# Reading the moving tiles of the weight products backwards, and spacing one activation buffer by 32 bytes per tile

## The reference

```python
def conv_glu_ffn(h, w_gate, w_up, conv_w, conv_b, w_down):
    g = h @ w_gate
    ...
    return (jax.nn.silu(gc) * (h @ w_up)) @ w_down

x = x + jnp.concatenate([y_pool, y_mla, y_mem], axis=-1) @ w_o[l]
x = x + conv_glu_ffn(rms_norm(x, g_ffn[l]), w_gate[l], w_up[l], conv_w[l], conv_b[l], w_down[l])
```

## Time and profile before

| what | value |
|---|---|
| median of 3 runs | 1601.56 us (1597.0 to 1602.5) |
| span of the profiled execution, first to last instruction | 1599.0 us |
| the profiled execution's own time around the span | not given; the median of the runs is 2.6 us more than the span |
| TensorE matmul busy | 1573.0 us (98%) |
| VectorE busy | 1154.1 us (72%) |
| ScalarE busy | 862.4 us (54%) |
| moved by DMA | 331 MB, mean 207 GB/s |

### The profile page before, as it was taken

The page is one execution under the profiler, slowest core; times in us unless marked ns, Lnnn a source line. Parts: engine busy times, 40 slices in busy tenths (PEclk is TensorE's granted clock), DMA queues, the critical chain, the costliest instruction groups (busy, mean ns, idle before and its releaser), DMA issues.

```text
span 1599.0 us, 24289 instructions
## 1 busy us (share of the span) xinstructions
PE 1573.0 (98%) x9650; PEld 1400.7 (88%) x9650; DVE 1154.1 (72%) x1696; ACT 862.4 (54%) x1321; POOL 151.6 (9%) x164
## 2 busy tenths in 40 slices
PE   8998999989999999999999999999999999999999
PEld 6787889988999999988799888888888888888887
DVE  6797867877778886759778777777777777455544
ACT  6855546767665555655556454544444444444442
POOL 0000000321221220034213000000000000000000
PEclk9999999999999999999999999999999999999999
DMA  9999975533457774343244545555455454555552
GB/s 373 369 343 349 365 285 209 188 114 121 180 189 267 285 272 179 132 158 132 97 144 178 189 170 199 184 186 210 172 197 191 179 211 175 205 199 185 198 196 105
DMA packets 47825, 331.02 MB, mean 207 GB/s; under 512 B 5281, under 2 KB 6689, under 8 KB 8417
## 3 DMA queue, kind: packets, MB, share of 16 engines
q1 hardware_dynamic: 45184, 312.20, 53.5%
q0 software_dynamic: 2240, 17.04, 2.8%
q10 hardware_dynamic: 290, 0.25, 0.1%
HBM read 327.37 MB, written 2.10 MB: 206 GB/s over the span
## 4 chain that ended last, share of the span: by engine, by line
PE 89%; DVE 5%; DMA 3%; ACT 2%; issue 1%; POOL 0%; SPq 0%; ACTq 0%; DVEq 0%; POOLq 0%
PE ps L1173 20%; PE ps L1174 11%; PE ps L1169 9%; PE ps L1170 8%; PE ps L1171 8%; PE ps L1228 5%; PE ps L1227 5%; PE ps L1226 5%; PE ps L1216 4%; PE ps L1217 3%; PE ps L1218 3%; DVE wl L1916 2%; DMA raw<-in_wts 1%; DMA xs<-in_xN 1%; PE ps L1384 1%; PE ps L1351 1%
## 5 line engine op out<-in xcount | busy, mean ns | idle before, releaser
L1916 DVE TENSOR_TENSOR wl<-raw,wh 128x1024 fp32r<-128x1024 f32 x512 | 626.2, 1236 | 282.4 <-ACT wh L1519 281.9
L1519 ACT ACTIVATE wh<-raw 128x1024 fp32r<-128x1024 f32 x512 | 531.3, 1054 | 377.2 <-PE ps L1228 130.6
L1173 PE MATMUL ps<-hA,wh 128*128 128x512 f32 x1408 | 488.7, 390 | 0.0
L1174 PE MATMUL ps<-hA,wl 128*128 128x256 f32 x1408 | 397.0, 282 | 0.0
L1173 PEld LDWEIGHTS ps<-hA,wh 128*128 128x128 f32 x1408 | 264.2, 188 | 55.3
L1174 PEld LDWEIGHTS ps<-hA,wl 128*128 128x128 f32 x1408 | 266.1, 189 | 0.0
L1169 PE MATMUL ps<-hA,wh 128*128 128x256 f32 x752 | 219.5, 292 | 0.0
L1170 PE MATMUL ps<-hA,wh 128*128 128x256 f32 x752 | 211.7, 282 | 0.0
L1171 PE MATMUL ps<-hA,wl 128*128 128x256 f32 x752 | 211.7, 282 | 0.0
L1169 PE MATMUL ps<-hB,wh 128*128 128x256 f32 x576 | 164.4, 285 | 0.8 <-DVE work L2362 0.4
L1170 PE MATMUL ps<-hB,wh 128*128 128x256 f32 x576 | 161.1, 280 | 0.0
(11 more groups left out here) (303 smaller groups left out, 2077.9 us busy)
## 6 DMA issues: line engine op xcount, KB each, us to landing
raw<-in_wts SPq DMA_DIRECT2D x256, 1024.0 KB, 4.8
raw<-in_ada SPq DMA_DIRECT2D x36, 1024.0 KB, 6.1
side<-in_ada POOLq DMA_DIRECT2D x12, 1024.0 KB, 8.5
work<-in_memN SPq DMA_DIRECT2D x2, 1024.0 KB, 8.9
xs<-in_xN POOLq DMA_DIRECT2D x1, 2048.0 KB, 20.6
xs<-in_xT POOLq DMA_DIRECT2D x2, 1024.0 KB, 7.8
out_rows<-xs SPq DMA_DIRECT2D x8, 256.0 KB, 2.4
wp<-in_dt SPq DMA_DIRECT2D x8, 128.0 KB, 2.7
```

What stands on the lines that cost most here:

```text
L1173: e.matmul(ps[bank][:, :], w1, hl, start=first, stop=False)
L1174: i = e.matmul(ps[bank][:, T:2 * T], w2, hl[:, 0:T], start=False, stop=last)
L1519: e.activation(wh[:, h % WS, :], raw[:, n % RAW, part * HALF:(part + 1) * HALF], ACT.Copy).then_inc(s_hi)
L1916: e.tensor_tensor(wl[:, h % WS, :], src, wh[:, h % WS, :].bitcast(F32), ALU.subtract).then_inc(s_lo)
```

## The change

Every moving tile of the weight products is addressed from its last column with a step of -1. Where the weights are stationary, the output tile in PSUM is addressed backwards too, so each column lands where it did. Where the weights move, the output stays forward, and the host stores each group of 512 weight columns in reverse in HBM instead (`standing` tells which groups). The loads of stationary blocks keep their addresses and their step.

The second edit puts 8 elements (32 bytes) between the K-tiles of `hA` and `hA2` (class `Slots`), so that tile kt begins at 128 + 32 kt or 160 + 32 kt modulo 512; `hB` and `hB2` are not spaced. The 480 bytes for it come out of the mask table, which is stored without its unused halves (576 in place of 1024 bytes per partition), and out of a gap ahead of `hB`, which is aligned to 512 in place of 2048 bytes. Everything behind `hA` moves by 480 or 512 bytes, `work` by 64.

The number and the order of the instructions on all five engines are the same; the one row that differs is the load of the masks.

```diff
+class Slots:
+    def __getitem__(self, at):
+        rows, kt, w = at
+        first = kt * (512 + SHIFT)
+        return self.tensor[rows, first + w.start:first + w.stop]
...
-        hA = sb("hA", [P, KT, 512], F32R)
+        hA = Slots(sb("hA", [P, KT * 512 + SHIFT * (KT - 1)], F32R))
...
-        at[0] += (hA_off - at[0]) % 2048
+        at[0] += (hA_off - at[0]) % 512
...
-        mk = sb("mk", [P, len(LEVELS), P], U8, 1)
+        mk = sb("mk", [P, P + 64 * (len(LEVELS) - 1)], U8, 1)
...
-        hA2 = nc.alloc_sbuf_tensor_at("hA2", [P, KT, 512], F32R, offset=hA_off + 32)
+        hA2 = Slots(nc.alloc_sbuf_tensor_at("hA2", [P, KT * 512 + SHIFT * (KT - 1)], F32R, offset=hA_off + 32))
...
-                hl = moving[buf][:, kt % KT, :]
+                hl = moving[buf][:, kt % KT, 0:512]
...
-                    e.matmul(po, w1, hl[:, 0:T], start=first, stop=False)
-                    e.matmul(po, w1, hl[:, T:2 * T], start=False, stop=False)
-                    i = e.matmul(po, w2, hl[:, 0:T], start=False, stop=last)
+                    po, hi, lo = (x[:, ::-1] for x in (po, hl[:, 0:T], hl[:, T:2 * T]))
+                    e.matmul(po, w1, hi, start=first, stop=False)
+                    e.matmul(po, w1, lo, start=False, stop=False)
+                    i = e.matmul(po, w2, hi, start=False, stop=last)
                 else:
-                    e.matmul(ps[bank][:, :], w1, hl, start=first, stop=False)
-                    i = e.matmul(ps[bank][:, T:2 * T], w2, hl[:, 0:T], start=False, stop=last)
+                    e.matmul(ps[bank][:, ::-1], w1, hl[:, ::-1], start=first, stop=False)
+                    i = e.matmul(ps[bank][:, T:2 * T][:, ::-1], w2, hl[:, 0:T][:, ::-1], start=False, stop=last)
...
-                w1, w2 = (w[:, h % WS, c % 2 * 512:c % 2 * 512 + 512] for w in (wh, wl))
+                w1, w2 = (w[:, h % WS, c % 2 * 512:c % 2 * 512 + 512][:, ::-1] for w in (wh, wl))
...
+            if not standing(kind, wn, cols) and j % 4 == 3:
+                wts[nw, :, (j - 3) * P:(j + 1) * P] = wts[nw, :, (j - 3) * P:(j + 1) * P][:, ::-1].copy()
```

More of the change, by code:

```diff
@@ L27 @@
 LANES = 6
+SHIFT = 8
 SETS = (tuple(c + P * j for c in (6144, 6656, 2048, 2560) for j in range(4)),
@@ L832, in order, with __init__ @@
     return o
+class Slots:
+    def __init__(self, tensor):
+        self.tensor = tensor
+    def __getitem__(self, at):
+        rows, kt, w = at
+        first = kt * (512 + SHIFT)
+        return self.tensor[rows, first + w.start:first + w.stop]
 class Counts:
@@ L1141, in _ @@
                 elif b[0] == "consts":
-                    e.dma_start(mk[:].rearrange("p a b -> p (a b)"), msk).then_inc(s_mask, 16)
+                    e.dma_start(mk[:], msk).then_inc(s_mask, 16)
                     e.dma_start(cs[:, P:], cst[:, P:]).then_inc(s_const, 16)
@@ L1182, in m @@
                 for j, kt in enumerate(kts):
-                    w1, w2 = wh[:, h % WS, j * 512:(j + 1) * 512], wl[:, h % WS, j * 512:(j + 1) * 512]
+                    w1, w2 = (w[:, h % WS, j * 512:(j + 1) * 512][:, ::-1] for w in (wh, wl))
                     if fresh[j]:
@@ L1203, in chunk @@
                     c = 2 * pair + i
-                    w1, w2 = wh[:, h % WS, i * 512:(i + 1) * 512], wl[:, h % WS, i * 512:(i + 1) * 512]
+                    w1, w2 = (w[:, h % WS, i * 512:(i + 1) * 512][:, ::-1] for w in (wh, wl))
                     if kt == kts[0]:
@@ L2042, in pick @@
                         src = bank[:, :].rearrange("p (a w) -> p a w", a=4)
-                        mask = mk[:, 0, :].unsqueeze(1).broadcast_to([P, 4, P])
+                        mask = mk[:, 0:P].unsqueeze(1).broadcast_to([P, 4, P])
                     else:
@@ L2048, in pick @@
                         src = bank[:, 0:T].rearrange("p (a n w) -> p a n w", a=4, w=h)
-                        mask = mk[:, li, 0:64].rearrange("p (n w) -> p n w", w=h).unsqueeze(1).broadcast_to([P, 4, n, h])
+                        mask = mk[:, P + 64 * (li - 1):P + 64 * li].rearrange("p (n w) -> p n w", w=h).unsqueeze(1).broadcast_to([P, 4, n, h])
                     e.copy_predicated(dst, mask, src).then_inc(mark(t, "dve", ("p", li)))
@@ L2561, in constants, with standing @@
             m[:, n, 0:64] = (s // (2 * h) == late // (2 * h)) & (s % (2 * h) < h)
-    return c, m.reshape(P, -1)
+    return c, np.concatenate([m[:, 0]] + [m[:, n, 0:64] for n in range(1, len(LEVELS))], 1)
+def standing(kind, wn, cols):
+    if kind == "m" or wn == "w_down_2":
+        return False
+    return wn != "w_kv_up_2" or cols[0] % 256 == 0
 def kernel(**inputs):
```

## The result

The kernel became slower: 1619.3 us (median of 4 runs, 1616.9 to 1621.9) against 1601.4, a ratio of 1.013 with a 95% interval of 1.011 to 1.014. The forecast was 1547, the range 1518 to 1640 held the time, and the case to which I gave the most chance was wrong in its sign.

A forecast was written before the change was run, and what follows sets the result against it. Behind 200 us the kernel was taken as a TensorE matmul queue, number times spacing. Reading backwards gave -55 us, spacing, output, reversal and masks 0: 1601.6 - 55 = 1547 us, range 1518 to 1640.

The forecast's parts named there:

- the case to which I gave the most chance: Whole kernel: faster by 55 us, to 1547 us within 1535 to 1568; chance 0.43.
- The columns' own 106.7 and 213.3 ns: TensorE matmuls: at the full 2.4 GHz clock, 256 columns take 106.7 ns and 512 take 213.3.
- The excess is the same for 256 and 512 columns, so it belongs to something that happens once per matmul: Matmul spacings: excess about 13.5 ns in both shapes, assigned to loading the next stationary block; 113 us in all.
- Collisions: SBUF: the excess is the load's read colliding with the moving tile's; at most 91 us can go.
- reading backwards: Moving tiles: running the load's way gives a third as many collisions, two thirds of excess above 2.5 ns gone; -55 us.
- The spacing of the K-tiles: `hA` tiles: spacing changes each tile's distance to the weight block, not the number of passings; 0 us, within 5.7 either way.
- The sign that was named for a distance that matters beyond the direction: Timeline after: `hA` tiles whose spacing goes with kt would show that distance matters beyond direction; no size given.
- The output backwards, the reversal, the masks: PSUM output, host's weight reversal and mask load: columns land in their old places, reversal precedes launch; 0 us.
- A: Moving tile held behind the load, in all `hB2` and some `hA` matmuls: +45 us, 1647; chance 0.23.
- B: Excess is the load's own share in any direction; only `hA` products gain, about -6 us, 1596; chance 0.17.
- C: All matmuls: excess falls to the transposes' 2.5 ns because spacing keeps reads apart, -83 us, 1519; chance 0.12.
- D: Backward tiles move at half pace; if only backward-output matmuls do, 876 us more, about 2480; chance 0.05.

The follow-up runs named there:

- mb3_kinds: None of the kernel's work: matmul groups varying type, distance and address against the next loaded block; bf16 512 columns took 215.8 ns, 256 took 109.2.
- mb2_maps: None of the reference's work: the kernel's pair and triple patterns at distances in 16-byte steps, then columns 128 to 512; forward pair 346.7 ns at 32, triple 360.0 at 0.
- mb1_pairs: None of the reference's work: 2472 matmuls in groups of 32 varying direction, distance and block; 512 columns at distance 0 took 226.7 ns forward, 233.3 backward.
- e_back: Against the kernel before: everything read backwards, in the old layout, K-tiles not spaced; 1612.4 us, ratio 1.009 (1.007 to 1.011).
- e_space: Against the kernel before: K-tiles of `hA` spaced, masks as in the changed kernel, all read forwards; 1602.3 us, ratio 1.002 (1.001 to 1.004).
- mb4_starts: None of the kernel's work: 16 triples or pairs follow one matmul of 16 to 512 columns; at distance 192, spacings of 113.3 and 117.8 ns.

## Why the prediction was wrong, point by point

- *What bounds the kernel*: right. The time is the number of matmuls times their spacing; both before and after TensorE is full behind 200 us, and its waits stayed as short (the longest 5.5 us in both).
- *The columns' own 106.7 and 213.3 ns*: right. No row of before shows them; mb3_kinds does (106.6 ns for 256 more bf16 columns), and it shows the 2.5 ns over them too. Plain float32 goes at half that pace in the kernel before: four matmuls of 256 columns in 1.03 us (L1384 at 622.73), (1.03 - 0.38)/3 = 217 ns each, against 109 for the 128 of the transposes, so 0.84 ns a column against 0.42. The load's 107 was my estimate from the transposes; the nearest to it is L101 of mb2_maps, where fp32r matmuls of 128 and of 192 columns, with a block of 128 loaded beside each, both take 112 ns ((2.40 - 0.27)/19 and (2.73 - 0.27)/22).
- *"The excess is the same for 256 and 512 columns, so it belongs to something that happens once per matmul"*: this is the step that failed. mb2_maps shows 12 ns over at 256 columns and 19 at 512 in the same place, mb3_kinds 2.5 ns in bf16 with the same number of columns and a load beside each. It goes mostly with fp32r columns. Distance 0, where I compared them, is the worst place of 256 columns (120.0 ns) and the best of 512 (227.1), and only there are the two equal.
- *Collisions*: my guess, and wrong way round. The loads out of `hA` in the narrow products to 506 us took 192 ns on average at distance 0 (L1169) and 188 after (L1183), so load and tile do bear on each other; no run shows in what way. I read the 3.7 ns between `hA` and `hA2` as fewer collisions. A forward tile of 512 columns at the right place takes less beside its load (226.7 ns at distance 0); a backward one gets nothing back (233.3 ns at all eight distances of mb1_pairs). So the step that took the reads running the same way to meet a third as often, and two thirds of the excess to go with that, failed: the -55 us of *reading backwards*, the largest term, is +6.2 us in gate and up's line (e_back), about +7 in the down product, 1 to 5 in the input product and -1 in the narrow ones, +14 in the whole (ratio 1.009).
- *The spacing of the K-tiles, 0 within 5.7 us either way*: the whole stayed inside the bounds (e_space +0.24%, 3.9 us), the reason was not there. It took gate and up off distance 32, +5.8 us, more than the bound by itself, and gave 2.4 us back in the `hA` triples (359.7 to 355.0 ns). The sign that was named for a distance that matters beyond the direction, a spacing that goes with kt, is there in after: pairs from 349.2 to 357.5 ns.
- *The output backwards, the reversal, the masks, 0*: right; L88 of mb1_pairs shows the output (227.1 ns against 226.7).
- *Rivals*: A named a slower result, by a lock at `hB2`. `hB2` stayed at 118.0 ns, so A is out though it had the sign, and no run shows a tile held to the pace of a load. B had the excess unmoved by direction. C and D are out: no line went near 2.5 ns over or to half pace. The case that came true, that the old layout stands where forward reading is favoured and any change loses that, wasn't among them. The rows to suspect it were there: rows 5 to 7 showed that place alone moves the excess, which says that a place can be lost as well as won.

## What to carry to other kernels

Where fp32r matmuls stood back to back here, their spacing depended on where the moving tile lies, modulo 256 bytes, against the block loaded beside it (226.7 to 234.3 ns for 512 columns, 113.3 to 120.0 for 256, forward in mb1_pairs), and, most of all at 512 columns, on direction (226.7 forward and 233.3 backward at distance 0): measure a map of your own pattern first, give every buffer one constant place from it, read forwards, and expect part of the gain only, since one place can have two rhythms (340.0 and 353.3 ns a triple at 192 in mb4_starts). Before an excess is put down "once per matmul", vary the columns at one place and the type; two shapes that agree at one place (13.3 ns over at distance 0) can differ at another (11.9 and 19 at 128). And the busy time of a line whose matmuls overlap with those of other lines isn't their spacing (0.28 us long and 118.0 ns apart out of `hB2`): take the starts. A tuned time may rest on a lucky place, so an edit that moves addresses by 32 bytes (226.7 to 233.3 ns for 512 columns) is a change of its own and has to be tested alone.

## What the runs showed of the hardware that I had not expected

- At a constant distance fp32r moves 512 columns in 226.7 to 234.3 ns (mb1_pairs), bf16 in 215.8 (mb3_kinds); 256 in 113 to 121 against 109.1.
- A backward moving tile of 512 fp32r columns took 233.3 ns at all eight constant distances of mb1_pairs; where the distance changed from tile to tile, backward pairs took 349.2 to 357.5 (after). A backward output cost nothing (227.1 ns against 226.7).
- The time given back at distance 0 was 6.7 ns with a block of 128 columns, 3.3 with 64, 1.7 with 32 (mb1_pairs).
- Forward triples at distance 192 ran at 340.0 or 353.3 ns, steadily, as the matmul ahead of them had it (mb4_starts). What in the engine keeps the rhythm stays open. So does whether the gift needs a load and a tile that run opposite ways (no run turned the load around), and why a tile and block that travel together by 32 bytes alternate between 226 and 236 ns.
